# A ring of 16 expert slots in place of 12, its new slots laid over tensors of the state-space layer and of the router

## What is computed

```python
h = h + swa_sink_attention(rmsnorm(h), ...)
h = h + swiglu(rmsnorm(h), ffn_w_gu, ffn_w_down)          # 1024 -> 2 x 3584 -> 1024
h = h + mamba2_ssd(rmsnorm(h), ...)                       # gated, normed, then y @ w_out
hn = rmsnorm(h)
top_v, top_i = top_k(hn @ w_router, 2)                    # 2 of 8 experts for each token
for e in range(8):
    h = h + combine[..., e] * (silu(hn @ w_gate[e]) * (hn @ w_up[e])) @ w_down[e]
out = rmsnorm(h)
```

## Time and profile before

| what | value |
|---|---|
| median of three runs | 1438.44 us |
| the profiled execution | 1437.92 us |
| its span, from the first to the last instruction | 1436.2 us |
| TensorE matmul busy | 1360.0 us, 95% of the span |
| VectorE, ScalarE, GpSimd busy | 30%, 27%, 5% |
| mean granted TensorE clock | 0.994 of full speed |
| moved in all | 465.34 MB, 324 GB/s over the span |

### The profile page before, as it was taken

The page is one execution under the profiler, slowest core; times in us unless marked ns, Lnnn a source line. Parts: engine busy times, 40 slices in busy tenths (PEclk is TensorE's granted clock), DMA queues, the critical chain, the costliest instruction groups (busy, mean ns, idle before and its releaser), DMA issues.

```text
span 1436.2 us, 30954 instructions
## 1 busy us (share of the span) xinstructions
PE 1360.0 (95%) x13543; PEld 812.3 (57%) x13543; DVE 425.9 (30%) x646; ACT 383.5 (27%) x575; POOL 69.4 (5%) x116
## 2 busy tenths in 40 slices
PE   8999999999999999999989999999879999999775
PEld 7788888887999985345243354344233354345232
DVE  7775545456689954000000000000000000001102
ACT  6664344346588843001000000000000000000001
POOL 2042000000002221000000000000000000000000
PEclk9999999999999999999999999999999999999998
DMA  9369655556543446999999999999999999999994
GB/s 349 119 231 407 212 182 187 188 174 183 156 131 123 172 170 259 407 401 380 414 420 425 413 420 424 414 420 421 416 420 425 414 419 424 414 412 393 412 420 193
DMA packets 131117, 465.34 MB, mean 324 GB/s; under 512 B 9680, under 2 KB 35552, under 8 KB 114608
## 3 DMA queue, kind: packets, MB, share of 16 engines
q1 hardware_dynamic: 123808, 440.44, 78.5%
q0 software_dynamic: 4832, 15.56, 2.8%
q10 hardware_dynamic: 2352, 7.44, 1.5%
HBM read 447.28 MB, written 16.12 MB: 323 GB/s over the span
## 4 chain that ended last, share of the span: by engine, by line
PE 62%; DMA 15%; issue 11%; SPq 6%; DVE 2%; POOLq 2%; ACT 1%; DVEq 1%; POOL 0%; ACTq 0%
PE bank L1333 25%; PE bank L1351 13%; DMA e_ring<-moe_w_gu_in 9%; PE bank L838 7%; PE bank L840 7%; PE bank L839 7%; SPq L368 5%; DMA e_ring<-moe_w_down_in 5%; POOLq L467 1%; PE bank L1324 1%; DMA ring<-swa_w_qkv_in 1%; DVE w_lo L1464 1%; POOLq L465 0%; PE bank L1060 0%; ACT w_hi L525 0%
## 5 line engine op out<-in xcount | busy, mean ns | idle before, releaser
L1333 PE MATMUL bank<-e_ring,xgT 128*32 128x384 f32 (+1 forms) x5376 | 522.2, 542 | 29.5 <-DMA e_ring<-moe_w_gu_in 29.4
L1333 PEld LDWEIGHTS bank<-e_ring,xgT 128*32 128x32 f32 x5376 | 167.6, 110 | 377.0 <-issue 290.1
L1464 DVE TENSOR_TENSOR w_lo<-ring,w_hi 128x2048 fp32r<-128x2048 f32 (+1 forms) x84 | 191.8, 2287 | 108.7 <-ACT w_hi L525 108.4
L525 ACT ACTIVATE w_hi<-ring 128x2048 fp32r<-128x2048 f32 (+1 forms) x84 | 159.1, 1896 | 127.1 <-PE bank L840 118.8
L2020 DVE TENSOR_TENSOR m_hh<-m_sg,bank 128x512 f32<-128x512 f32 (+1 forms) x42 | 23.7, 616 | 530.9 <-PE bank L1333 530.9
L1351 PE MATMUL bank<-e_ring,m_hT_a 128*32 128x256 f32 x2688 | 151.6, 385 | 12.8 <-DMA e_ring<-moe_w_down_in 12.8
L838 PE MATMUL bank<-w_hi,hT_hi 128*128 128x512 f32 (+1 forms) x336 | 130.9, 390 | 2.6 <-DVE w_lo L1464 2.2
L1351 PEld LDWEIGHTS bank<-e_ring,m_hT_a 128*32 128x32 f32 x2688 | 90.5, 111 | 71.7 <-issue 17.2
L840 PE MATMUL bank<-w_hi,hT_lo 128*128 128x512 f32 (+1 forms) x336 | 129.2, 385 | 0.0
L839 PE MATMUL bank<-w_lo,hT_hi 128*128 128x512 f32 (+1 forms) x336 | 129.1, 384 | 0.0
L1351 PE MATMUL bank<-e_ring,m_hT_b 128*32 128x256 f32 x2016 | 113.0, 380 | 11.7 <-DMA e_ring<-moe_w_down_in 11.7
(11 more groups left out here) (360 smaller groups left out, 1228.5 us busy)
## 6 DMA issues: line engine op xcount, KB each, us to landing
e_ring<-moe_w_gu_in SPq DMA_DIRECT2D x128, 1024.0 KB, 17.0
e_ring<-moe_w_gu_in SPq DMA_DIRECT2D x128, 768.0 KB, 20.4
e_ring<-moe_w_down_in SPq DMA_DIRECT2D x96, 1024.0 KB, 18.0
ring<-ffn_w_gu_in SPq DMA_DIRECT2D x28, 1024.0 KB, 5.6
e_ring<-moe_w_down_in SPq DMA_DIRECT2D x32, 512.0 KB, 15.4
ring<-ffn_w_down_in SPq DMA_DIRECT2D x14, 1024.0 KB, 4.9
xg_rows<-zeros POOLq DMA_DIRECT2D x36, 256.0 KB, 13.4
ring<-ssm_w_in_in SPq DMA_DIRECT2D x8, 1024.0 KB, 5.0
```

Source lines behind the costliest of these rows:

```text
L525: act.activation(w_hi[:, m % SPLIT, 0:w], ring[:, m % RING, 0:w], ACT.Copy).then_inc(hi_ready, 1)
L1333: ins = pe.matmul(bank[banks[b]][quad, 0:w], xgT[:, k, rows], e_ring[:, c % ERING, block_n * w:(block_n + 1) * w], start=(k == 0), stop=(k ...
L1464: dve.tensor_tensor(w_lo[:, m % SPLIT, 0:w], ring[:, m % RING, 0:w], w_hi[:, m % SPLIT, 0:w].bitcast(F32), ALU.subtract).then_inc(lo_ready, 1)
```

## The change

`ERING` becomes 16. The list `SLOT_OF` says which slot of SBUF ring position r is: positions 0 and 1 are slots 13 and 14 of `e_ring`, which now runs on over `hT_hi` and `hT_lo`; position 2 is a tile of its own, `e_last`, over the state-space layer's `acc`, `Xdt` and `arg`; positions 3 to 14 are the twelve slots of before; position 15 is slot 12, over `hT`. The positions over `ring` use the semaphores of `ring`'s slots, with what these count before the experts added to the wait. In `build`, SP's first loads of expert 0 become sixteen, in another order of waits. In all expert code `e_ring[:, c % ERING ...]` becomes `e_slot(c)`.

```diff
-ERING = 12
+ERING = 16
+SLOT_OF = (13, 14, 15, 0, 1, 2, 3, 4, 5, 6, 7, 8, 9, 10, 11, 12)
...
-        e_ring, = phase(e_ring=((ERING, SLOT), F32))
+        e_ring, = phase(e_ring=((ERING - 1, SLOT), F32))
...
-        e_loaded = [sem(f"e_loaded{r}") for r in range(ERING)]
...
+        e_loaded = [(slot_loaded[SLOT_OF[r]], loads_until(MOE0 - RING + SLOT_OF[r])) if SLOT_OF[r] < RING else
+                    (sem(f"e_loaded{r}"), 0) for r in range(ERING)]
...
+        _, _, e_last = phase(
+            under_z=((G, TT, 256), F32), under_yT=((KI, T), F32), e_last=((SLOT,), F32))
...
+        def e_slot(c):
+
+            r = SLOT_OF[c % ERING]
+            return e_ring[:, r] if r < ERING - 1 else e_last
...
-                dst = e_ring[:, c % ERING, 0:n].rearrange("p (k n) -> p k n", k=src.shape[1])
-                sp.dma_start(dst, src).then_inc(e_loaded[c % ERING], 16)
+                dst = e_slot(c)[:, 0:n].rearrange("p (k n) -> p k n", k=src.shape[1])
+                sp.dma_start(dst, src).then_inc(e_loaded[c % ERING][0], 16)
...
+            sp.wait_ge(chunk_used, SO0)
+            for c in range(2):
+                expert_load(0, c)
+            sp.wait_ge(c_y, G)
+            expert_load(0, 2)
             for c in range(RING):
                 sp.wait_ge(lo_ready, MOE0 + c - RING + 1)
-                expert_load(0, c)
-            for c in range(RING, ERING):
-                sp.wait_ge(chunk_used, MOE0 + (c - RING) % SPLIT - SPLIT + 1)
-                expert_load(0, c)
+                expert_load(0, 3 + c)
+            for c in range(2 * SPLIT):
+                sp.wait_ge(chunk_used, MOE0 + c % SPLIT - SPLIT + 1)
+                expert_load(0, 3 + RING + c)
+            sp.wait_ge(r_mm, 4)
+            expert_load(0, ERING - 1)
 
             sp.wait_ge(r_order, 1)
...
                     each = LAYER_CHUNKS // ERING * 16
-                    pe.wait_ge(e_loaded[c % ERING], it * (E * each) + (p * each + 16 * (c // ERING + 1)))
+                    loaded, before = e_loaded[c % ERING]
+                    pe.wait_ge(loaded, it * (E * each) + (before + p * each + 16 * (c // ERING + 1)))
...
-                                            e_ring[:, c % ERING, block_n * w:(block_n + 1) * w],
+                                            e_slot(c)[:, block_n * w:(block_n + 1) * w],
...
-                                                    e_ring[:, (32 + c) % ERING, (k - k0) * D + d * 256:(k - k0) * D + (d + 1) * 256],
+                                                    e_slot(32 + c)[:, (k - k0) * D + d * 256:(k - k0) * D + (d + 1) * 256],
```

## The result

The changed kernel takes 1429.89 us, the median of 9 runs (1426.82 to 1435.06); the kernel before takes 1438.44 us, the median of 9 (1436.62 to 1442.59). Between the medians lie 8.6 us, where 9.9 were forecast. The ratio, estimated from all runs, is 0.993 with a 95% interval of 0.991 to 0.995; the quotient of the two medians, 0.9941, lies in it. The profiled execution took 1426.82 us, its span is 1425.1 us; before, they were 1437.92 and 1436.2. That is why I read the gain mostly from times inside a profile.

A forecast was written before the change was run, and what follows sets the result against it. Slots hold back loads in expert 0; from about 672 us the DMA's remaining bytes bound the kernel. Four slots save 9.9 us, other terms zero: 1438.44 - 9.9 = 1428.5 us, range 1424.0 to 1434.0 us.

The forecast's parts named there:

- The bound: Expert 0 is bound by TensorE, its loads held back by slots; from about 672 us bytes left decide the end.
- rival B: At 672 to 681 us, a deeper ring smooths the joint release of four slots: 1.9 us more, 1426.6 us; chance 0.07.
- Item 1: At the end of expert 0, four more chunks are loaded, 4.19 MB at 422 GB/s: 9.9 us gained.
- its cap: In expert 1, TensorE's work limits the gain: 12.5 us by the nearer row, 19.6 by the other.
- at least 81.8 us of work: TensorE's work in expert 1: its 94.3 us less 12.5 us idle time.
- the other bound: Expert 1's work as two thirds of expert 0's 112.1 us, 74.7 us, capping the gain at 19.6 us.
- Items 2 to 5: Before and early in expert 0: first three loads, queued ring loads, sixteenth load and `gain_row` all cost nothing.
- rival C: Before 672 us, the sixteenth load might not count: three chunks, 7.5 us, 1431.0 us; chance 0.07.
- Item 7: From 672 to 1420 us, up to 15 transfers in flight: 1.8 us with either sign, taken as zero.
- A: In the expert loads, more slots raise the rate and all 53.9 us of waiting go: 1384.5 us; chance 0.01.
- E: From 672 to 1420 us, more transfers in flight cost rate, 7.5 us per 1%; 1450.9 us at 3%; chance 0.05.
- D: From 491 to 561 us, prefetch slows the output projection, expert 0 starts late: no change, 1438.4 us; chance 0.08.

The follow-up runs named there:

- the two mirror kernels: Changed kernel with lead 12 for loads waiting on expert 0, 16 later: 1438.53 us; with lead 16 for experts 0 and 1, 12 later: 1429.42 us.
- the split kernel: Changed kernel with the last four down chunks of three-group experts given free one by one, the last two together: 1426.91 us, again 1428.26 us.

## Why the prediction was right

The forecast was 1428.5 us in a range of 1424.0 to 1434.0, the measured median is 1429.89.

**The bound.** Slot-bound in expert 0, DMA-bound from 672 on: shown. The landing time of 645 to 669 is 6.8 us after (6.7 before); the new ring is full at the end of expert 0, as the old one was. GB/s in 645 to 672 were to stay near 395: they are 406, and 416 and 418 in two more profiles of the changed kernel, while 563 to 672 as a whole has 389 before and 387 after. The nine microseconds behind have 358 against 334. Both are small, and in the direction of rival B. What failed is a part of the sentence that the DMA "is never let go idle" up to 1414 us: behind experts 3 and 6 the ring of 12 held it back a little, as shown above.

**Item 1, four slots for 9.9 us.** At expert 2 the profiles have 10.2 to 10.8 us (206.5 less 196.3 to 195.7), the medians of three sets 8.6, 9.1 and 12.1. The term was well sized, and its cap was not reached, with 5.8 us of idle time left in expert 1. But the forecast that this idle time would fall to 2.6 us was wrong. It was worked out as 12.5 - 9.9, as if each microsecond of lead took one from the waits behind 697 us. In the rows, TensorE is idle for 12.5 us in 697 to 767 before, and 5.8 in 697 to 757 after, 6.7 less, while the expert is 10.2 us shorter. The rest was counted as work. Both stretches have 762 matmuls, busy for 57.49 us before and 54.22 after, 3.3 us less, at a clock of 0.98 and 0.97; 6.7 + 3.3 = 10.0 of the 10.2 us. The reason is most likely that a starved TensorE works in spurts, one chunk at each landing, and the profile counts the modelled tail of each as busy. The waits of the kernel before in 697 to 767:

```profile
PE bank L1351 <- DMA e_ring<-moe_w_down_in: 7.2, 6, 3.5
PE bank L1333 <- DMA e_ring<-moe_w_gu_in: 5.3, 15, 0.5
```

These are 21 stops, where the changed kernel has 5 in 697 to 757. There a chunk of 16 gate matmuls between two stops counts as 1.50 us and two chunks in a row as 2.79, one down chunk as 1.93 and two as 3.66; so a stop adds about 0.2 us: an estimated 16 x 0.2 = 3.2 us of busy time less. So "at least 81.8 us of work" was no floor: by the same count expert 1 now has 757.41 - 673.06 - 5.8 = 78.6 us of it. The idle time is too low as a measure of what a lead can save. How good the other bound is, 19.6 us by two thirds of expert 0's work, was not tried.

**Items 2 to 5, loads moved ahead at no cost.** Expert 0 starts at 561.09 (560.91 before). The twenty microseconds by which the first ring loads are later cost nothing. How little the start of the last four matters was not foreseen. The prediction had called the sixteenth load the tightest (rival C); with chunks 12 to 15 some 11 us late (issued from 560.51 us on, the sixteenth last of all), the run does not lose what a median can show.

**Item 7, a deeper queue.** Taken as zero, give or take 1.8 us: 416 GB/s over 647 us before and after, and 418 and 416 in the two mirror kernels. It is not quite zero in the profiles. From the start of expert 2 to the end of the span the three with a lead of 12 there take 668.6 to 669.1 us, and six with 16 take 666.3 to 667.7; the seventh is the split kernel's 678.5. So a lead of 16 behind expert 2 may be worth 1 to 2 us, in line with the 1.7 us above. That is not shown: the medians can't tell so little (1429.42 with a lead of 12 there, 1429.2 with 16, on the same chip), and the profile with a lead of 14 has 671.1, not a time in between. The stake was "up to 15 transfers in flight", and the runs don't come to that. In 700 to 760 us of the changed kernel, where TensorE starves, SP waits only 2.4 us for slots, but its issues follow each other at the pace of the DMA (13 in 29.79 us from 710.64 on). Loads of 1024 KB issued in 720 to 730 land after 18.0 us and those of 750 to 760 after 28.2; at 421 GB/s that is an estimated 7 and 11 in flight. What holds SP's issues up there was not tried. Rivals A and E fall with this, D with the start of expert 0, and C, three slots for 7.5 us, with the 10.2 to 10.8 us at expert 2.

**The sum.** Behind expert 2 the profiles differ by more than the four slots' term: the last chunk lands at 1408.8 us (1410 was forecast), 11.1 us earlier, of which 10.0 are there at expert 2. The extra microsecond is of the size that the lead of 16 brings behind expert 2, and also of the size by which single executions scatter; the runs do not separate the two. The medians of the same two kernels lay 8.6, 9.1 and 12.1 us apart, so the mechanism was right, and how near a single median comes to the forecast is luck within some 2 us.

## What to carry to other kernels

Where a stream of loads runs at the DMA's full rate nearly to the end, as here, count the bytes that are still to be loaded at the moment when it becomes the bound. Here a buffer was worth its bytes divided by that rate, once, where the loads were held back by slots, and little anywhere else. Tell a DMA that waits for slots from one that is full by the time from issue to landing together with GB/s, not by the busy share. Before working to start loads earlier, check whether the stretch behind has slack to make up for it; here the depth at the end of one expert was nearly all that mattered.

## What the runs showed of the hardware that was not expected

The DMA's share is 1.01 at 395 GB/s, held back by slots, and 1.02 at 421, full: it is no measure of saturation here. The time from issue to landing of a 1 MB load grew with the length of the queue at an unchanged rate: 14.0 us before and 22.8 us after in expert 3, both inside stretches of 416 GB/s. A lead of 12 left the DMA at 334 to 359 GB/s in the nine microseconds behind the joint release of four slots after experts 0 and 6, with shares of 0.95 and 0.98. And expert 0 had more room in the DMA than the prediction used: asked for it, the DMA moved 415 GB/s there in place of 389, beside a TensorE that took 111.95 us for the expert, as in every other profile (111.95 to 111.97).
